# A fused decoder layer on one core: GpSimd splits, the weighted x, the sparse rows' pieces and the low gate parts of the last stage, rearranged

## What is computed

```python
s = jnp.einsum('thpd,hpkd->thpk', q, sub_keys)           # 8 heads, 2 halves, 128 keys
... top 16 of each half, top 16 of the 256 sums -> experts, gates (128 per token)
u = jnp.take(expert_u, eb, axis=0)
act = jax.nn.gelu(jnp.einsum('tkd,td->tk', u, xb), approximate=False)
v = jnp.take(expert_v, eb, axis=0)
return jnp.einsum('tk,tkd->td', gb * act, v)
```

## Time and profile before

| | us |
|---|---|
| median of 3 runs | 1900.07 (1898.75 to 1901.19) |
| profiled execution, its own time | 1896.21 |
| its span | 1894.4 |
| first V matmul | 1237.2 |
| last V matmul | 1880.5 |

### The profile page before, as it was taken

How to read it: one execution, slowest core, us unless ns; L and a number is a source line. 1 busy time by engine, 2 the same in 40 slices (tenths; PEclk the granted TensorE clock), 3 DMA queues, 4 the chain that set the end, 5 groups by cost and what they waited for, 6 DMA issues and landing times.

```text
span 1894.4 us, 33463 instructions
## 1 busy us (share of the span) xinstructions
PE 1872.1 (99%) x11798; PEld 1759.1 (93%) x11798; DVE 1387.4 (73%) x2303; ACT 944.8 (50%) x1342; POOL 1237.3 (65%) x538
## 2 busy tenths in 40 slices
PE   9999999999999999999999999999999999999997
PEld 7888889888999999999999999989999999999997
DVE  8544685035635777958888888269999989999987
ACT  6453355474544444544444444445555555555555
POOL 3867768877898999999999999952222214343301
PEclk9999999999999999999999999999999999999999
DMA  8544646564754665655555555689999989999984
GB/s 331 188 144 147 200 145 223 192 193 158 213 180 179 219 213 209 208 204 200 195 198 198 198 199 199 210 303 359 394 390 377 371 348 350 375 380 385 384 305 143
DMA packets 83299, 473.99 MB, mean 250 GB/s; under 512 B 9630, under 2 KB 12574, under 8 KB 38302
## 3 DMA queue, kind: packets, MB, share of 16 engines
q1 hardware_dynamic: 65288, 367.30, 54.5%
q0 software_dynamic: 12384, 90.18, 12.2%
q10 hardware_dynamic: 5552, 15.51, 2.7%
HBM read 468.07 MB, written 4.19 MB: 249 GB/s over the span
## 4 chain that ended last, share of the span: by engine, by line
PE 52%; POOL 29%; issue 10%; DVE 4%; DMA 4%; ACT 1%; POOLq 0%; DVEq 0%; SPq 0%; ACTq 0%
POOL wlo L466 28%; PE ps L2021 16%; PE ps L1915 15%; PE ps L2026 8%; PE ps L1920 8%; DMA raw<-in_w_v 3%; DVE wlo L1468 2%; PE ps L1931 1%; PE ps L1615 1%; PE ps L1617 1%; ACT whi L566 1%; PE ps L1616 1%; POOL wlo L500 1%; DVE x_back L1478 0%; DVE gather_low L1478 0%
## 5 line engine op out<-in xcount | busy, mean ns | idle before, releaser
L566 ACT ACTIVATE whi<-raw 128x1024 fp32r<-128x1024 f32 x691 | 732.5, 1060 | 917.6 <-PE ps L1920 348.2
L466 POOL TENSOR_TENSOR wlo<-raw,whi 128x1024 fp32r<-128x1024 f32 x428 | 1036.9, 2432 | 193.7 <-ACT whi L566 187.6
L1915 PE MATMUL ps<-x_parts,whi 128*128 128x428 f32 x2048 | 577.5, 363 | 0.0
L2021 PE MATMUL ps<-gate_parts,whi 128*128 128x428 f32 x2000 | 567.7, 365 | 3.0 <-DVE gate_parts L1470 2.9
L1920 PEld LDWEIGHTS ps<-x_parts,wlo 128*128 128x128 f32 x2048 | 384.0, 188 | 17.8 <-POOL wlo L466 2.1
L2026 PEld LDWEIGHTS ps<-gate_parts,wlo 128*128 128x128 f32 x2000 | 374.9, 188 | 17.9 <-POOL wlo L500 3.1
L1920 PE MATMUL ps<-x_parts,wlo 128*128 128x214 f32 x2048 | 382.5, 268 | 1.4 <-POOL wlo L466 1.4
L2026 PE MATMUL ps<-gate_parts,wlo 128*128 128x214 f32 x2000 | 373.3, 268 | 2.0 <-POOL wlo L500 2.0
L1468 DVE TENSOR_TENSOR wlo<-raw,whi 128x1024 fp32r<-128x1024 f32 x248 | 302.7, 1221 | 44.9 <-ACT whi L566 44.5
L1915 PEld LDWEIGHTS ps<-x_parts,whi 128*128 128x128 f32 x2048 | 310.5, 191 | 0.0
L2021 PEld LDWEIGHTS ps<-gate_parts,whi 128*128 128x128 f32 x2000 | 302.7, 191 | 6.6 <-issue 2.3
(11 more groups left out here) (260 smaller groups left out, 2094.7 us busy)
## 6 DMA issues: line engine op xcount, KB each, us to landing
raw<-in_w_u SPq DMA_DIRECT2D x128, 1024.0 KB, 4.8
raw<-in_w_v SPq DMA_DIRECT2D x128, 1024.0 KB, 8.7
raw<-in_w_front SPq DMA_DIRECT2D x180, 512.0 KB, 3.6
big<-in_mem ACTq DMA_DIRECT2D x8, 256.0 KB, 6.3
big<-in_mem_t ACTq DMA_DIRECT2D x2, 1024.0 KB, 6.2
big<-in_x ACTq DMA_DIRECT2D x2, 1024.0 KB, 7.2
x_back<-x2t_scratch ACTq DMA_DIRECT2D x2, 856.0 KB, 10.0
big<-in_x_t SPq DMA_DIRECT2D x3, 512.0 KB, 7.8
```

The source lines that it names most:

```text
L466: nc.gpsimd.tensor_tensor(wlo[:, j % SPL, :], raw[:, j % RAW, :], whi[:, j % SPL, :], ALU.subtract).then_inc(lo_done, 1)
L566: nc.scalar.activation(whi[:, (base + j) % SPL, :], raw[:, (base + j) % RAW, :], ACT.Copy).then_inc(hi_done, 1)
L1915: nc.tensor.matmul(sums[:, 0:2 * TD], whi[:, s, cols], x_parts[:, :, m, 0:TD], start=m == 0, stop=False, skip_group_check=True)
L2021: nc.tensor.matmul(sums[:, 0:2 * TD], whi[:, s, cols], gate_parts[:, g, :, 0:TD], start=False, stop=False, skip_group_check=True)
```

## The change

There are four parts.

1. GpSimd's low parts at V's opening go from eight to four (`OPENING` 8 to 4). Its first three gathers then stand in a row behind the fourth; VectorE writes `wlo` from piece 4 on.
2. The weighted x is formed in place in `X_GAINED`, in two halves. ACT issues the three DMAs of x and the first half of the gain before the last four highs of U, the second half behind V's first high and behind a wait for the first product (`half_gained`). VectorE multiplies the first half behind the third-last `take_chunk` of U (`gained_half(0)`), the second behind piece 4 of V.
3. U rows stand behind pieces 5 to 122 (before 15 to 118), V rows behind 128 to 236 (before 128 to 233). The groups are added behind 245, 247 and 251 (before 240, 241 and 251), and the DMAs that serve them move 6, 4 and 7 pieces later on ACT.
4. `gate_parts` has four buffers for three, ACT writes the high gate part one piece ahead, and VectorE writes the low gate parts of two pieces in one instruction (2x214 columns), behind the `wlo` of the even piece. Semaphore counts follow, and a few small statistics columns are placed anew.

```diff
-SPL = 3
+SPL, GPL = 3, 4
...
-OPENING, SPARE_BLOCKS, VECTOR_LOW = 8, 5, 8
+OPENING, SPARE_BLOCKS, VECTOR_LOW = 4, 5, 8
...
-ROWS_FROM, WEIGHTS_AT_PIECE, ROWS_UNTIL = 15, 127, 234
-ADDED_AT = (*range(240, 239 + GROUPS), 251)
+ROWS_FROM, WEIGHTS_AT_PIECE, ROWS_UNTIL = 5, 127, 238
+ADDED_AT = (*range(245, 243 + 2 * GROUPS, 2), 251)
...
-        return ROWS_FROM + n * (WEIGHTS_AT_PIECE - 6 - ROWS_FROM) // PER
+        return ROWS_FROM + n * (WEIGHTS_AT_PIECE - 2 - ROWS_FROM) // PER
...
+            act.wait_ge(picks, 1)
+            for g in range(GROUPS):
+                act.dma_start(X_GAINED[g * TS:(g + 1) * TS, :], x2_dram).then_inc(x_s_in, 16)
+            load_half_gain(0)
             for j in range(NK // CHUNKS_PER_BODY * BODY, 2 * NK):
                 high(j, 0, U0)
...
             high_v(0, 0)
+            act.wait_ge(half_gained, 1)
+            load_half_gain(1)
             gelu_in_place(0, NK - 2)
...
-                if j == 3:
-                    for g in range(GROUPS):
-                        act.dma_start(X_S[g * TS:(g + 1) * TS, :], x2_dram).then_inc(x_s_in, 16)
-                if j == 6:
-                    act.dma_start(X_GAINED, gain_rows[0].partition_broadcast(P)).then_inc(gain_s_in, 16)
-                gated_high(0, j)
+                gated_high(0, j + 1)
...
-                dve.wait_ge(ghi_done, j + 1)
-                nc.vector.tensor_tensor(gate_parts[:, j % SPL, 1, 0:TD], W[:, j % NK, :], gate_parts[:, j % SPL, 0, 0:TD],
-                                        ALU.subtract).then_inc(glo_done, 1)
+                if j % 2 == 0:
+                    dve.wait_ge(ghi_done, j + 2)
+                    two = slice(j % GPL, j % GPL + 2)
+                    nc.vector.tensor_tensor(gate_parts[:, two, 1, :], W[:, j % NK:j % NK + 2, :], gate_parts[:, two, 0, :],
+                                            ALU.subtract).then_inc(glo_done, 1)
...
+            def gained_half(h):
+                dve.wait_ge(x_s_in, 16 * GROUPS)
+                dve.wait_ge(gain_s_in, 16 * (h + 1))
+                part = X_GAINED[0:GROUPS * TS, h * (D // 2):(h + 1) * (D // 2)]
+                nc.vector.tensor_tensor(part, part, HALF_GAIN[0:GROUPS * TS], ALU.mult).then_inc(half_gained, 1)
+
             for k in range(takes_done, NK - 1):
                 take_chunk(0, k, TOK_PAIRS)
                 if k + 2 < NK - 1:
                     join(0, k + 2)
+                if k == NK - 3:
+                    gained_half(0)
             v_step(0, split=False)
             join(0, NK - 1)
             take_chunk(0, NK - 1, TOK_PAIRS)
-            v_step(1, split=False)
...
-                if j == 13:
-                    dve.wait_ge(x_s_in, 16 * GROUPS)
-                    dve.wait_ge(gain_s_in, 16)
-                    filled = slice(0, GROUPS * TS)
-                    step(nc.vector.tensor_tensor(X_GAINED[filled], X_S[filled], X_GAINED[filled], ALU.mult))
+                if j == 4:
+                    gained_half(1)
```

More of the change, by code:

```diff
@@ L171 @@
 LATE_AT = XG_AT + D
-assert SK_AT <= SEL_AT and SUMS_AT + 2 * PER <= TK_AT and LATE_AT + ACT_BANKS * TD <= GAIN_AT
+HALF_GAIN_AT = LATE_AT + ACT_BANKS * TD
+assert SK_AT <= SEL_AT and SUMS_AT + 2 * PER <= TK_AT and HALF_GAIN_AT + D // 2 <= GAIN_AT
 SS, VAR, ROOT, R = 0, 10, 20, 30
@@ L760, in gated_high @@
             def gated_high(k0, j):
-                nc.scalar.activation(gate_parts[:, j % SPL, 0, 0:TD], W[:, k0 + j, :], ACT.Copy).then_inc(ghi_done, 1)
+                nc.scalar.activation(gate_parts[:, j % GPL, 0, :], W[:, k0 + j, :], ACT.Copy).then_inc(ghi_done, 1)
             high_v(0, 0)
+            act.wait_ge(half_gained, 1)
+            load_half_gain(1)
             gelu_in_place(0, NK - 2)
@@ L810, in _ @@
                     high_v(i, j)
-                    gated_high(i * BODY - NK, j)
+                    gated_high(i * BODY - NK, j + 1)
             for j in range(BODY):
                 high_v(LAST_BODY - 1, j)
-                gated_high((LAST_BODY - 1) * BODY - NK, j)
-                if j == 8:
+                gated_high((LAST_BODY - 1) * BODY - NK, j + 1)
+            for j in range(BODY):
+                high_v(LAST_BODY, j)
+                gated_high(LAST_BODY * BODY - NK, j + 1)
+                if j == 0:
+                    load_back(1)
+                if j == 2:
                     act.wait_ge(rows_taken, 2 * PER)
@@ L818, in _ @@
                     load_addend(1)
-            for j in range(BODY):
-                high_v(LAST_BODY, j)
-                gated_high(LAST_BODY * BODY - NK, j)
-                if j == 0:
-                    load_back(1)
-                if j == 3:
+                if j == 7:
                     for k in range(2, GROUPS):
@@ L1993, in _, with v_block @@
                 u_piece(U_BODIES, j)
-            def v_block(s, c, first=False, last=False):
+            def v_block(piece, c, first=False, last=False):
                 cols = slice(c * P, (c + 1) * P)
-                g = (s - V0) % SPL
-                nc.tensor.matmul(ps[:, c, 0:2 * TD], whi[:, s, cols], gate_parts[:, g, :, 0:TD],
+                s, g = (V0 + piece) % SPL, piece % GPL
+                nc.tensor.matmul(ps[:, c, 0:2 * TD], whi[:, s, cols], gate_parts[:, g, :, :],
                                  start=first, stop=False, skip_group_check=True)
-                return nc.tensor.matmul(ps[:, c, TD:2 * TD], wlo[:, s, cols], gate_parts[:, g, 0, 0:TD],
+                return nc.tensor.matmul(ps[:, c, TD:2 * TD], wlo[:, s, cols], gate_parts[:, g, 0, :],
                                         start=False, stop=last, skip_group_check=True)
             def v_ready(i, j, low=True):
-                pe.wait_ge(glo_done, i * BODY + (j + 1))
+                pe.wait_ge(glo_done, i * (BODY // 2) + (j // 2 + 1))
                 if low:
@@ L2014, in v_piece @@
                 s = (V0 + j) % SPL
-                g = (s - V0) % SPL
+                g = j % GPL
                 for pair in ((first + q) % 4 for q in range(4)):
@@ L2025, in v_piece @@
                     for cols, sums in both:
-                        ins = nc.tensor.matmul(sums[:, TD:2 * TD], wlo[:, s, cols], gate_parts[:, g, 0, 0:TD],
+                        ins = nc.tensor.matmul(sums[:, TD:2 * TD], wlo[:, s, cols], gate_parts[:, g, 0, :],
                                                start=False, stop=False, skip_group_check=True)
@@ L2041, in _ @@
                     pe.wait_ge(act_taken, NK)
-                ins = v_block(V0 % SPL, c, first=True)
+                ins = v_block(0, c, first=True)
             ins.then_inc(used, 1)
@@ L2062, in _ @@
                         pe.wait_ge(first_joined, c + 1)
-                    ins = v_block((V0 + j) % SPL, c, first=j > last_first, last=j == last_first)
+                    ins = v_block(FOLD_BODY * BODY + j, c, first=j > last_first, last=j == last_first)
                     if j == last_first and c < 7:
```

43 lines of the change are left out of this document (25 added, 18 removed).

## The result

| | before | after |
|---|---|---|
| median, runs side by side | 1898.83 (1895.1 to 1901.19) | 1904.92 (1901.48 to 1910.52) |
| profiled execution | 1896.21 | 1901.48 |
| its span | 1894.4 | 1899.7 |

The ratio of after to before is 1.0038, 95% interval [1.0027, 1.0049]: slower by 7 us, where 1898.0 was forecast and the range ended at 1903.0. The page's parts that answer to the earlier trace rows hardly tell the two apart. VectorE is busy 15 us less, GpSimd 19 us less, and PE 3 us more.

A forecast was written before the change was run, and what follows sets the result against it. PE was taken to set the time nearly everywhere, with only 15.0 us of V's losses to win back. Terms of +2.4, +0.2, -3.0, -1.6, +3.8, +0.2, -2.6, -1.3, -0.1, -0.3, +0.2 gave -2.1: 1898.0 us from 1900.07, range 1891.5 to 1903.0.

The forecast's parts named there:

- The change touches nothing before piece 252 of U.: Front and most of U: no effect before about 1221 us, so only V's 15.0 us of losses can be won back.
- V starts late, +2.4: U's end: early x load delays V's first weights and half gain, so PE starts V 2.4 us later (bounds 0.5, 4.4).
- Case A: Rival: smooth opening, V's weights in time (+0.5 for 2.4), row 0 lands in 6 us; 1892.9 us, chance 0.32.
- GpSimd's waits -3.0: V's opening: with four GpSimd splits, three PE waits behind them go, 3.0 of the 5.2 us lost there.
- the x load -1.6: V's opening: x load, half the gain load and the product leave it, giving 1.6 of the remaining 2.2 us back.
- Row 0, +3.8: V piece 6: row 0's gather lands late and PE loses 3.8 us, 2.5 with the fastest landing, 10.9 with the slowest.
- Case B: Rival: row 0 takes the trace's 14.5 us from issue instead of 7.4, +7.1; 1905.1 us, chance 0.14.
- First rows -2.6: V's first rows, 101 steps: wider spacing and paired gate parts lighten VectorE, 2.6 of 4.1 us back (bounds 1.0, 3.8).
- Case C: Rival: no effect in the rows, whose losses come from transfers, not VectorE; 1901.9 us by that alone, chance 0.14.
- V rows -1.3: V's second rows: more slack for VectorE per row, 1.3 of 2.8 us back (bounds 0.3, 2.3).
- fold -0.1: V's fold: one low gate part leaves the stretch ahead of six reductions PE waits for, 0.1 us back.
- end -0.3 and +0.2: V's end: VectorE's last chain loses one low gate part, 0.3 us back; groups added behind 245 and 247 lose 0.2.

The follow-up runs named there:

- before_128: Kernel before with only an idle filler made longer (96 columns for 64), moving x_parts up by 128 bytes; ratio 1.0022.
- after_placed: Kernel after with the small stats buffer allocated behind gather_low, so x_parts lies 512 bytes below its old place; ratio to before 0.9986.
- x_a_body_earlier: placed_rows9 with the loads of x and the half gain issued 16 U pieces ahead of U's end instead of 4; ratio to before 0.9985.
- only_four: Kernel before with part 1 alone: GpSimd splits four V pieces instead of eight; ratio 1.0006.
- before_x_early: Kernel before with part 2 alone: weighted x formed at U's end in two halves, rows unmoved; ratio 0.9999.
- placed_rows9: after_placed with U rows from piece 9 instead of 5; ratio to before 0.9976.
- rows9_again: Same instructions as placed_rows9, run once more beside the kernel before; ratio 0.9973.
- before_again: Kernel before run again beside itself with no edit; ratio 0.9994.
- after_again: Kernel after run again with no edit, on the same chip as before; ratio to before 1.0028.
- only_pairs: Kernel before with part 4 alone (paired low gate parts, four buffers), stats placed as in after_placed; ratio 0.9996.
- pairs_four: Kernel before with parts 1 and 4 together, placed as only_pairs; ratio 0.9991.

## Why the prediction was wrong, point by point

- **"The change touches nothing before piece 252 of U."** This is the step that failed. Its instructions hardly change there (one small VectorE instruction on the statistics becomes two), but the place of an operand does. The front is longer by 5.4 us in the profiled executions (571.2 to 576.6), and the placement is worth 0.0022 to 0.0052 in the ratios (before_128 at one end, after against after_placed at the other). No term, rival or bound of the prediction had it. Without it the forecast's -2.1 of 1896 us, a ratio of 0.9989, stands beside after_placed's 0.9986: the sum for V was near, but by luck as much as by working: its errors cancel, as the next points show.
- **V starts late, +2.4.** Right in its mechanism: 3.4 more lost in pieces 0 to 3 than before in one execution and 1.9 in the other. The half clock, which only the first of them had, is the difference of some 1.5. The chain ran as told but for the product, which was ready in time. Case A's way out (transfers in time, +0.5) does not follow from the transfers alone: x_a_body_earlier brought them in time, and the upper bound of that same step, a product held behind GpSimd's split, took over.
- **GpSimd's waits -3.0 and the x load -1.6.** Right only as a sum. Apart they gave 0 (only_four) and, with the later start of V counted, 0 (before_x_early). Together, with the paired gate parts and with the rows from piece 9, the opening's loss went from 5.2 to 0.4 and -0.1 (placed_rows9, rows9_again); no run has the two alone. Costing them one by one assumed that the second wait wasn't hidden behind the first.
- **Row 0, +3.8.** Right in its mechanism, and near in landing (7.8 us for 7.4) and PE's wait (3.28). Undersized by the half clock: piece 6 lost 5.1 and 5.6. Case B did not come, though the time measured, 1904.9, is almost its 1905.1: it asked for a row that takes 14.5 us and a loss of 10.9 at piece 6.
- **First rows -2.6 (bounds 1.0 to 3.8).** About right. Before and before_again lost 3.9 and 5.1, after and after_again -0.4 and -0.6, but that pair flatters: the five kernels with before's instructions lose 3.7 on the mean, the eight with all four parts 0.8 (-0.8 to 3.0). Of these 2.9 some 0.6 to 0.8 is a faster pace (below), which the sum did not have. That VectorE's load is behind the rest, as said, and not the fewer transfers asked for, is not shown: no run spaces the rows alone, and only_pairs and pairs_four (2.7 and 2.1) are within the scatter. Case C, no effect in the rows, did not come.
- **V rows -1.3, fold -0.1, end -0.3 and +0.2.** V rows: 0.6 and 0.8 back against each twin, which is what the faster pace gives over 107 pieces (0.6), so the wider spacing gave nothing that shows. The fold lost 4.4 and 4.5 for 2.9 and 3.8. PE waits there for a reduction that stands behind the first V row in VectorE's order, and the granted clock is 0.57 in the 4 us behind it:

```profile
PE ps L2017 <- DVE x_back L1524: 1.1, 1, 1.1
...
1564.00:1568.00 4.00, 2.92 (x16) 2.08 (x15) 4.00 (x7) 1.54 (x3) 0.93 (x1) 1.00 0.68 233
1568.00:1572.00 4.00, 4.00 (x15) 3.54 (x15) 4.00 (x7) 1.08 (x2) 0.00 (x0) 0.57 0.89 340
```

  It is a toss that the change does not decide: eight of the seventeen kernels' traces have the low clock there and lose 3.6 to 5.0 in pieces 122 to 136, before_again among them; the nine others have full clock and lose 2.6 to 3.1. In the last ten pieces 0.7 more was lost than before, 0.6 of it at piece 248, just behind the second group's sum, for the 0.2 forecast. The tail behind PE's last V piece is 0.3 shorter (18.2 for 18.5), as forecast.
- **The range** took in only what V could do. It was 1.9 us short of the time. The chances of its two lists differ by a little: forecast and C, both within 0.2%, make 0.54, where 0.52 is given.

## What to carry to other kernels

An edit that resizes a buffer moves every buffer allocated behind it. Where a matmul reads one of them, compare the pace of a stage that the edit doesn't touch, and pad to the old place modulo 256 bytes before judging the edit itself. Two waits that hide each other are one term: here taking either away gave nothing, so price them as a pair. And a PE wait of some 3 us has a second price, the slow stretch behind it, so a row or a product is best placed where its data is surely there: four pieces later took 5 us off this kernel, and 2 to 3, within the noise, off the one placed as before.
